# Hybrid SSD and sparse-attention layer: reciprocals on their own, a head's maximum ahead of the last head's scaling, gate units spread, constant matmuls in the prefix's waits

## The reference

```
shift, scale, gate = split(c @ w_ada + b_ada, 3)
h      = rmsnorm(x, g_pre) * (1 + scale) + shift
z, xbc, dt, q, kv, nsa_gate, z_att, merge_gate = split(h @ w_in)
y_ssm  = (rmsnorm_4_groups(ssd(silu(conv4(xbc)), dt) * silu(z)) * g_ssm) @ w_ssm_out
y_nsa  = (attention(q, kv, nsa_gate) * silu(z_att)) @ w_nsa_out
merged = sigmoid(mg0) * y_ssm + sigmoid(mg1) * y_nsa
out    = x + gate * rmsnorm(merged @ w_out, g_post)
```

## Time and profile before

| what | value |
|---|---|
| median of 3 runs | 468.28 us (466.88 to 468.32) |
| the profiled execution's own time | 467.49 us |
| its span, first to last instruction | 465.6 us |
| PE busy | 436.6 us (94%) |
| DVE busy | 349.9 us (75%) |
| ACT busy | 271.3 us (58%) |
| POOL busy | 187.6 us (40%) |
| mean granted TensorE clock | 0.986 |

### The profile page before, as it was taken

How to read it: one execution, slowest core, us unless ns; L and a number is a source line. 1 busy time by engine, 2 the same in 40 slices (tenths; PEclk the granted TensorE clock), 3 DMA queues, 4 the chain that set the end, 5 groups by cost and what they waited for, 6 DMA issues and landing times.

```text
span 465.6 us, 9821 instructions
## 1 busy us (share of the span) xinstructions
PE 436.6 (94%) x3636; PEld 397.2 (85%) x3636; DVE 349.9 (75%) x617; ACT 271.3 (58%) x544; POOL 187.6 (40%) x188
## 2 busy tenths in 40 slices
PE   2679999999999999999899999989999999999995
PEld 2277999999999999987899888978989989899873
DVE  0384789999999999477778968587866669987733
ACT  3244796757667576556798744556564636534441
POOL 0154570013446346645375523344363332435430
PEclk9879999999999999999999999999999999999998
DMA  8999545364534544238756542424445224798102
GB/s 285 424 410 370 185 136 182 103 227 139 171 103 161 189 131 148 88 135 297 287 177 192 184 134 92 135 92 138 137 132 181 96 92 182 274 380 299 43 0 90
DMA packets 22390, 84.03 MB, mean 180 GB/s; under 512 B 2492, under 2 KB 2882, under 8 KB 21186
## 3 DMA queue, kind: packets, MB, share of 16 engines
q1 hardware_dynamic: 22344, 83.42, 51.0%
HBM read 82.36 MB, written 1.05 MB: 179 GB/s over the span
## 4 chain that ended last, share of the span: by engine, by line
PE 40%; DVE 6%; ACT 3%; issue 3%; DVEq 0%; ACTq 0%
PE gemm L716 9%; PE gemm L718 9%; PE gemm L717 9%; PE y_or_o L923 2%; ACT probs L1175 2%; PE score L887 1%; ACT w_hi L945 1%; DVE w_lo L1217 1%; PE score L889 1%; DVE probs L1493 1%; PE small L641 1%; PE small L643 1%; PE score L643 1%; PE score L642 1%; PE small L642 1%
## 5 line engine op out<-in xcount | busy, mean ns | idle before, releaser
L1562 POOL TENSOR_TENSOR w_lo<-w_raw,w_hi 128x256 fp32r<-128x256 f32 x85 | 108.3, 1275 | 170.0 <-ACT w_hi L945 154.2
L716 PE MATMUL gemm<-h_hi,w_hi 128*128 128x256 f32 x600 | 171.6, 286 | 2.5 <-DVE k_lo L1294 1.2
L1217 DVE TENSOR_TENSOR w_lo<-w_raw,w_hi 128x768 fp32r<-128x768 f32 (+1 forms) x117 | 132.1, 1131 | 48.3 <-ACT w_hi L945 47.8
L718 PE MATMUL gemm<-h_hi,w_lo 128*128 128x256 f32 x600 | 166.5, 278 | 0.0
L717 PE MATMUL gemm<-h_lo,w_hi 128*128 128x256 f32 x600 | 166.5, 278 | 0.0
L945 ACT CAST w_hi<-w_raw 128x1024 fp32r<-128x1024 f32 x117 | 122.3, 1046 | 43.4 <-PE gemm L718 22.2
L716 PEld LDWEIGHTS gemm<-h_hi,w_hi 128*128 128x128 f32 x600 | 113.0, 188 | 6.1 <-issue 2.8
L717 PEld LDWEIGHTS gemm<-h_lo,w_hi 128*128 128x128 f32 x600 | 112.9, 188 | 0.7 <-issue 0.2
L718 PEld LDWEIGHTS gemm<-h_hi,w_lo 128*128 128x128 f32 x600 | 112.9, 188 | 0.0
L1613 POOL TENSOR_TENSOR cb_decay<-decay,cb_T 128x512 f32<-128x512 f32 x8 | 15.0, 1874 | 72.5 <-ACT decay L1114 72.5
L716 PE MATMUL gemm<-ynorm_hi,w_hi 128*128 128x256 f32 x128 | 36.3, 283 | 1.0 <-DVE w_lo L1217 0.9
(11 more groups left out here) (252 smaller groups left out, 879.8 us busy)
## 6 DMA issues: line engine op xcount, KB each, us to landing
w_raw<-in_wpack SPq DMA_DIRECT2D x133, 512.0 KB, 3.5
w_ada_shift_scale<-in_w_ada SPq DMA_DIRECT2D x8, 1024.0 KB, 16.0
x_T<-in_xT SPq DMA_DIRECT2D x2, 512.0 KB, 6.1
x_residual<-in_x_tok SPq DMA_DIRECT2D x1, 1024.0 KB, 7.0
out_tok_dram<-out_tok SPq DMA_DIRECT2D x4, 256.0 KB, 2.1
ada_gate_products<-in_gate_bias SPq DMA_DIRECT2D x1, 512.0 KB, 4.3
g_post_rows<-in_g_post_rows SPq DMA_DIRECT2D x1, 512.0 KB, 5.9
consts<-in_consts SPq DMA_DIRECT2D x1, 272.0 KB, 22.0
```

What stands on the lines that cost most here:

```text
L716: nc.tensor.matmul(bank[:, 0:SEQ], w_hi, hi[:, k0 + k, :], start=first, stop=False)
L718: last = nc.tensor.matmul(bank[:, 0:SEQ], w_lo, hi[:, k0 + k, :], start=False, stop=end)
L1217: nc.vector.tensor_tensor(WL[:, n % LO_SLOTS, 0:c], RAW[:, u % RAW_SLOTS, 0:c], WH[:, n % HI_SLOTS, 0:c], ALU.subtract).then_inc(lo_ready, 1)
L1562: nc.gpsimd.tensor_tensor(WL[:, n % LO_SLOTS, c:1024], RAW[:, u % RAW_SLOTS, c:1024], WH[:, n % HI_SLOTS, c:1024], ALU.subtract).then_inc( ...
```

## The change

- The four reciprocals of the norm of y leave `yn` and become steps `rec` of their own, after the units w1k+1, w1k+3, w1v+3 and ks+5. The `yn`, `ynhi`, `ynlo` steps are placed anew: tiles 4 and 5 two to four units earlier, the last six at every second unit between the heads' steps.
- The order in a head's tile becomes q2(n+1), sc(n), pt(n-2), ex(n), ps(n-1); ex(n) moves up by one tile, and cs2 goes behind them in its tile.
- The eight `ag` units stand behind the ssm units 2, 4, 6, 8, 10, 12, 13, 14 and no longer behind each of 7 to 14; the DMA that seeds their sum moves up by two ssm units.
- PE multiplies constants (`keep_busy`, 128x128 by 256 columns, float32, result unused): 5 before the tile k = 6 of `ada_rows(0)`, 4 behind `ada_columns(0)`. `ada_columns(1)` comes after the first of unit 4's four row tiles, not after the second.
- POOL makes four of the eight tiles of `h` (k = 1, 3, 5, 7) and not two, and DVE subtracts tile k right after it has made, or waited for, `h`.

```
@@ -35,7 +35,7 @@
 PAIRS = ((("dtg", 0), ("b", 0)), (("kc", 0), ("b", 1)), (("kc", 1), ("b", 2)), (("vc", 0), ("b", 3)), (("vc", 1), ("c", 0)))
 PAIR_READ = (PAIRS[0], (("b", 1),), (("kc", 0), ("kc", 1), ("b", 2)), (("b", 3),), (("vc", 0), ("vc", 1), ("c", 0)))
 HALF_K = KT // 2
-GATE_FROM = 7
+GATE_BEHIND = (2, 4, 6, 8, 10, 12, 13, 14)
 
 
 def weight_units():
@@ -57,8 +57,8 @@
     units += [("mg", j, 0) for j in range(16)]
     for n in range(16):
         units += [("ssm", n // 2, n % 2)]
-        if GATE_FROM <= n < GATE_FROM + KT:
-            units += [("ag", 0, n - GATE_FROM)]
+        if n in GATE_BEHIND:
+            units += [("ag", 0, GATE_BEHIND.index(n))]
     units += [("nsa", j, 0) for j in range(8)] + [("out", j, 0) for j in range(8)]
     return units
 
@@ -123,8 +123,10 @@
     put(58, ("ssq", 1))
     tiles = TPG * SSM_GROUPS
     w1k, w1v, ks, q, mg = (UNITS.index((kind, 0, 0)) for kind in ("w1k", "w1v", "ks", "q", "mg"))
-    norm_units = [w1k + 1, w1k + 2, w1k + 4, w1k + 5, w1v + 4, ks, ks + 2, ks + 4, q + 1, q + 3, q + 5]
-    norm_units += [mg + n for n in (3, 5, 7, 8, 10, 11, 13)]
+    norm_units = [w1k + 1, w1k + 2, w1k + 4, w1k + 5, w1v + 1, w1v + 2, w1v + 4, ks + 2, ks + 4, q + 1, q + 3, q + 5]
+    norm_units += [mg + n for n in (4, 6, 8, 10, 12, 14)]
+    for g, u in enumerate((w1k + 1, w1k + 3, w1v + 3, ks + 5)):
+        put(u, ("rec", g))
     for j in range(tiles + 2):
         for ahead, name in ((2, "ynlo"), (1, "ynhi"), (0, "yn")):
             if 0 <= j - ahead < tiles:
@@ -143,18 +145,17 @@
         put(tiles[n], *steps)
 
     after_tile(q7 + 1, ("cs", 0), ("cs", 1))
-    after_tile(q7 + 2, ("cs2", 0))
     after_tile(q7 + 3, ("vt", 1))
     after_tile(q7 + 5, ("ct", 0), ("ct", 1))
     t0 = q7 - 2
     after_tile(t0 - 3, ("kpos", 0))
     for h in range(ATT_HEADS):
         after_tile(t0 - 2 + 2 * h, ("q2", h))
-    for h in range(ATT_HEADS):
-        after_tile(t0 + 2 * h, ("sc", h))
-        after_tile(t0 + 1 + 2 * h, ("ex", h))
-        after_tile(t0 + 2 + 2 * h, ("ps", h))
-        after_tile(t0 + 4 + 2 * h, ("pt", h))
+    for n in range(ATT_HEADS + 2):
+        for ahead, name in ((0, "sc"), (2, "pt"), (0, "ex"), (1, "ps")):
+            if 0 <= n - ahead < ATT_HEADS:
+                after_tile(t0 + 2 * n, (name, n - ahead))
+    after_tile(q7 + 2, ("cs2", 0))
     last_h = tiles.index(at(("mg", 15, 0)))
     for p in range(ATT_HEADS // 2):
         after_tile(t0 + 8 + 4 * p + (p == 0), ("pv", p))
@@ -249,7 +250,8 @@
     _last = [t for t in TILE_IDX if TILE_IDX[t] < TILE_IDX[_tile] and HOME[t][0] == HOME[_tile][0]]
     BEFORE[_tile] = _last[-2:] if _last and HOME[_last[-1]][1] == 1 else _last[-1:]
 RAW_SLOTS, HI_SLOTS, LO_SLOTS = 7, 4, 4
-H_POOL = (2, 6)
+H_POOL = (1, 3, 5, 7)
+KEEP_WARM = (5, 4)
 H_DVE = tuple(k for k in range(KT) if k not in H_POOL)
 EARLY_SPLITS = range(len(PAIRS), 17)
 OUT_K = 2
@@ -562,7 +564,7 @@
                     sp.dma_start(ALK[0:6].bitcast(mybir.dt.uint16), alibi_k).then_inc(al2_in, 16)
                 if u == UNITS.index(("mg", 0, 0)):
                     sp.dma_start(ALQ[0:6].bitcast(mybir.dt.uint16), alibi_q).then_inc(al_in, 16)
-                if u == UNITS.index(("ssm", 4, 0)):
+                if u == UNITS.index(("ssm", 3, 0)):
                     sp.wait_ge(yn_done, TPG * SSM_GROUPS)
                     sp.dma_start(AG[:], gate_bias).then_inc(ag_in, 16)
                 if u == UNITS.index(("nsa", 4, 0)):
@@ -588,9 +590,16 @@
                 last = nc.tensor.matmul(YB[:, 0:SEQ], cst("ones"), SQX[:, k, :], start=(k == 0), stop=(k == KT - 1))
             last.then_inc(ssx_full, 1)
 
+            def keep_busy(n):
+
+                for _ in range(n):
+                    nc.tensor.matmul(GB[2][:, 0:256], cst("ones"), CS[:, 0:256], start=True, stop=True)
+
             def ada_rows(s):
 
                 for k in range(KT):
+                    if s == 0 and k == KT - 2:
+                        keep_busy(KEEP_WARM[0])
                     if k % 2 == 0:
                         pe.wait_ge(ada_in[HALF_K * s + k // 2], 16)
                     for j in range(4):
@@ -610,6 +619,7 @@
             pe.wait_ge(bank_zeroed, 1)
             ada_rows(0)
             ada_columns(0)
+            keep_busy(KEEP_WARM[1])
 
             def begin_small(key):
                 n = T_IDX[key]
@@ -661,7 +671,7 @@
                         k = HALF_K * part + kk
                         if j == 0:
                             pe.wait_ge(h_ready, k + 1)
-                        if u == len(PAIRS) - 1 and kk == 2:
+                        if u == len(PAIRS) - 1 and kk == 1:
                             ada_columns(1)
                         for m in range(2):
                             c = 2 * kk + m
@@ -1358,9 +1368,7 @@
                     if k not in H_POOL:
                         nc.vector.tensor_scalar(HF[:, k, :], XT[:, k, :], AB[:, k:k + 1], shift(k), ALU.mult,
                                                 ALU.add).then_inc(h_f32, 1)
-                    if k > k0:
-                        h_lo(k - 1)
-                h_lo(k0 + HALF_K - 1)
+                    h_lo(k)
 
             scale_x(0)
             split_lo(0)
@@ -1430,11 +1438,12 @@
                     wait_y_out(dve, step)
                     x2 = XG[:, (i // 2) % 2, 2 * (i % 2):2 * (i % 2) + 2, :]
                     nc.vector.tensor_tensor(Z[:, 2 * i:2 * i + 2, :], x2, Z[:, 2 * i:2 * i + 2, :], ALU.mult).then_inc(ypre_done, 1)
+                elif what == "rec":
+                    wait_small_out(dve, ("ssq", i // 2, 0))
+                    root = RN[i // 2][:, i % 2, :]
+                    nc.vector.reciprocal(root, root).then_inc(recip_done, 1)
                 elif what == "yn":
                     if i % TPG == 0:
-                        g = i // TPG
-                        wait_small_out(dve, ("ssq", g // 2, 0))
-                        nc.vector.reciprocal(RN[g // 2][:, g % 2, :], RN[g // 2][:, g % 2, :]).then_inc(recip_done, 1)
                         dve.wait_ge(recip_done, i // TPG + 1)
                         dve.wait_ge(ysq_done, i // TPG + 1)
                     if i >= 2:
```

4 lines of the change are left out of this document (2 added, 2 removed).

## The result

The changed kernel takes 463.56 us (median of 4 runs, 461.92 to 464.84), the kernel before beside it 468.3 (4 runs): ratio 0.9916, 95% interval 0.9889 to 0.9943. By the ratio that is 3.9 us less, by the difference of the medians 4.7, by the spans of the two profiled executions (465.6 and 461.9) 3.7; the forecast was 8.7 less. The profiled execution took 463.74 us.

A forecast was written before the change was run, and what follows sets the result against it. The prediction called the kernel PE-bound with holes. Prefix 2.1, reciprocals 1.2, heads 4.3 and gate units 1.1 sum to 8.7 us, from 467.49 to 458.8, 459.6 as the runs' median; 8-in-10 range 457.3 to 464.3.

The forecast's parts named there:

- the reciprocals' term: Near 230 us: PE no longer waits for k_lo behind a reciprocal; gain 1.2 of 1.40 us, 0.2 given back.
- Prefix: Start of the kernel: constants hold the clock and transposes come earlier, so columns and unit 5 come earlier; gain 2.1 us.
- The idle piece: Sign for the prefix: PE would stand idle inside unit 4, with unit 5 at about 44.3 behind it.
- Rival 2: Prefix: the constants don't hold the clock and only the transposes' 0.7 us remain; 461.0 us, chance 0.13.
- a late fall costs little: Prefix, argument against the constants mattering: a late clock fall costs little, since the prefix's end hangs on unit 7.
- the cap is unit 7: Prefix: ACT copies the second sums only after rounding unit 7, whose raw weights end its idle time at 39.86.
- Rival 1: Prefix: POOL's tiles of h slow DVE's four second-half h_lo by 0.17 us each; 460.2 us, chance 0.10.
- Heads: Attention heads: the new order removes PE's waits for exponentials and scaling; 5.8 us less 1.5, gain 4.3.
- Rivals 3 and 5: Heads, ACT's queue: the first gives back half to all of 4.3 us (0.16), the second makes it slower, 470.9 (0.06).
- Gate units: Between ssm units: spreading the gate units removes PE's wait for w_lo; gain 1.1 us, bounds 0 and 1.3.
- the cover: Gate units: DVE's spare time per head, 7.9 us busy of 8.0 with one gate unit, so 0.1 us.
- rival 3: Heads: ACT's new wait before the exponentials makes w_hi and w_lo late; 463.9 us at full price, chance 0.16.

The follow-up runs named there:

- experiment 1: The changed kernel with the third reciprocal four units later, from behind w1v+3 to behind ks+3: 459.68 us, ratio 0.9826 to the kernel before.
- experiment 2: The changed kernel with six constant matmuls in PE's 2.9 us wait ahead of unit ks 1, the wait's cause untouched: 461.61 us, ratio 0.9867 to the kernel before.
- experiment 3: The changed kernel without its nine constant matmuls in the prefix: 463.31 us, ratio 0.9911 to the kernel before.
- experiment 10: The changed kernel with the third reciprocal four units later, the compressed scores in two places and unit 7's split behind the second sums: 456.47 us, ratio 0.9766.
- experiment 7: The kernel before with only the gate units spread and the seeding DMA moved up: 472.59 us, ratio 1.0106.
- experiment 6: The kernel before with only the reciprocals as steps of their own and the norm's steps placed anew: 469.32 us, ratio 1.0032.
- experiment 8: The kernel before with only the prefix part: constant matmuls, POOL's four tiles of h, DVE's order, transposes one tile earlier: 465.95 us, ratio 0.9958.

## Why the prediction was wrong

- **The failed step is the reciprocals' term.** The prediction had it at a gain of 1.2 us, bounds 0.3 and 1.4. It cost 4.1 in the changed kernel, 1.5 alone. The prediction saw that a reciprocal would stand in front of a read-out and priced that at 0.2, because ACT's tanh waits for it. It had the third in front of the keys' read-out; the third stands in front of the values', and the second, which it didn't price, in front of the keys'. And it didn't ask who else waits: PE, for the bank. PE's row at 223.94 shows no wait, and I took that for slack; the end of the read-out at 223.89, one row of DVE away, would have shown that there was none. The runs showed a wait of 2.9 us there: 1.7 went when the third was moved (experiment 1), and the 1.2 that stayed are the second's by the traces. Behind the wait came the low clock, half of the cost in experiment 2, which the term left out too. With this one step moved (experiment 1) the change gives 8.1 us and 459.68, where the forecast was 8.7 and 459.6.
- **Prefix, 2.1:** 1.8 by the two profiles, 2.0 alone. Every time on the way was met within 0.5 us (36.27 for 35.9, the columns 42.66 for 42.2, unit 5 44.44 for 44.3). The idle piece did move into unit 4. Part of the match is luck: the profile of before, from which the term was worked out, has the latest unit 5 of the five with the old prefix. Rival 2 was wrong about the clock, which the constants held up to unit 4 in all seven profiles that have them. Its argument that a late fall costs little isn't borne out either: without the constants the copy waits 1.56 us for PE (experiment 3). With them the cap is unit 7, as the prediction said (experiment 10).
- **Rival 1:** the four h_lo take 2.55 us (1.12 + 1.43), 0.32 more than before by my reading of the same four there (0.93 and 1.30), half of the rival's 0.68. By the Trainium skill (GPSIMD Engine Reference, Specifications), POOL and DVE contend when a DVE instruction has two SBUF inputs; the trace agrees in direction, 1.12 for the pair beside POOL's tiles of h, 0.93 for the same pair before. It is inside the 2.05 that unit 5 gained.
- **Heads, 4.3:** 4.4 alone, and 4.5 by the unit starts in the changed kernel, net of a fall of the clock that its profile has and that of before hasn't. Rivals 3 and 5, ACT's queue, didn't occur: no wait of PE for w_hi, none for w_lo above 0.2.
- **Gate units, 1.1:** 1.45 by the unit starts, but only 0.65 of it belongs to the spread; the rest is the heads' new order, which empties the same stretch. I had called the cover thin, "0.1; if it is gone, a part of the 1.1 comes back". In the old order the price isn't a part of 1.1 but 5 us (experiment 7). The prediction summed DVE's busy time per head, and a ring of waits between two engines doesn't show in such a sum.
- **The sum.** Of the 8.7 forecast, 3.9 came (0.84% of the kernel's time). The reciprocals are 5.3 off (4.1 lost for 1.2 gained); the other terms are together slightly better than forecast. 463.56 lies inside the range, at the price of rival 3, but by another mechanism than any of the rivals; that it does is luck.
- **Open:** why the clock falls in some waits and blocks and not in others like them; what the constants are worth by themselves, since in experiment 3 the clock differed in three places; and what moving the second reciprocal as well would give.

## What to carry to other kernels

Before an instruction is put ahead of another in a queue, look up on every engine who waits for the later one and subtract its end from the waiter's start: a wait of 0.0 in the list can mean no slack at all, and the cost of the delay then begins at its first tenth. When an experiment takes a part out and the time stays, look in the trace whether the part did nothing or whether something else changed by as much: in experiment 3 it was the second. On TensorE add what the idle time does to the clock behind it, which the list of waits doesn't show and the granted clock by stretch does. Parts of a change that share two engines' queues are to be tried together and apart; here one part was 5 us slower alone and harmless with another.

## What the hardware showed

- Waits of PE of much the same length did different things to the clock. The one of 2.9 us for `cmp_hidden` came with 6.8 us at 1.2 GHz in the changed kernel, one of 2.8 with 3.4 us (experiment 6), one of 2.9 with none (experiment 3). One of 1.2 us at the same place (experiment 1) came with none. In unit 4 one of 2.1 us was followed by 3.4 us at 1.2 GHz (experiment 2) and one of 1.9 by none (experiment 8).
- PE can fall to 1.2 GHz while it is busy all the time: at 3.72 us of products of 32 columns the granted clock fell to 0.50, for 3.4 us in the changed kernel and for 6.8 in experiment 1, in nine of ten profiles. Splitting them into 1.93 and 1.85 us, with wide matmuls in between, ended it in all three profiles that have it.
- Constant products need not be exact in time to hold the clock: with 2.81 us of them in a hole of 3.0 it stayed at 1.00 (experiment 2).
- A gate product (128x1024, DVE) took 1.28 us at 401.91 in the kernel before, where POOL's subtraction began after it, and 1.75 at 404.52 there and at 383.86 in experiment 7, where that was already running.
